# Feed-forward borders of a two-layer kernel: slots split at other times, sums of squares partly on GpSimd, chains in another order

## The reference, cut to what matters

```python
h = h + rmsnorm(mix, norm_mix_post)                 # end of the first layer's mixer
a = rmsnorm(h, norm_ffn_pre) @ w_ffn_in             # 1024 -> 2 x 2816
ap = jnp.pad(a, ((0, 0), (half, half), (0, 0)))
a = sum(ap[:, j:j + L] * conv_w[j] for j in range(CONV_W)) + conv_b
val, gate = a[..., :D_FF], a[..., D_FF:]
y = (jax.nn.gelu(gate, approximate=True) * val) @ w_ffn_out
h = h + rmsnorm(y, norm_ffn_post)
# second layer: u = rms_norm(h, norm_mix_2), u @ w_in_2 gives q, k, v of a windowed
# attention (q and k normalised per head and rotated), then the inputs of a recurrence
# (each a blend of a token with its two neighbours) and the gates
```

## Time and profile before

| what | value |
|---|---|
| median of 3 runs | 1938.53 us |
| lowest, highest | 1937.21, 1943.55 us |
| profiled execution, its own time | 1930.56 us |
| span of its trace | 1928.8 us |
| mean granted TensorE clock | 0.967 |
| ScalarE (ACT) busy | 649.8 us (34%) |
| GpSimd (POOL) busy | 88.5 us (5%) |
| DMA, mean over the span | 75 GB/s |

### The profile page before, as it was taken

The page is one execution under the profiler, slowest core; times in us unless marked ns, Lnnn a source line. Parts: engine busy times, 40 slices in busy tenths (PEclk is TensorE's granted clock), DMA queues, the critical chain, the costliest instruction groups (busy, mean ns, idle before and its releaser), DMA issues. The chain is left out here.

```text
span 1928.8 us, 38591 instructions
## 1 busy us (share of the span) xinstructions
PE 1771.6 (92%) x17168; PEld 1524.5 (79%) x17168; DVE 1020.2 (53%) x1527; ACT 649.8 (34%) x1064; POOL 88.5 (5%) x115
## 2 busy tenths in 40 slices
PE   6998999888999999989999998888579999999998
PEld 5888878888989989777677777777458888788877
DVE  3245765445635636546564555565656545353554
ACT  3242334433433423333334334333144322221232
POOL 7000000010000000100000000000001100000020
PEclk8999999979999999979999999999889999999999
DMA  5211120202222222221222200000052222223221
GB/s 163 88 67 45 63 81 23 90 23 88 87 88 88 96 101 88 90 80 66 77 83 71 77 24 4 4 4 10 2 229 88 88 89 106 90 88 109 88 88 66
DMA packets 29132, 144.57 MB, mean 75 GB/s; under 512 B 6315, under 2 KB 9659, under 8 KB 14380
## 3 DMA queue, kind: packets, MB, share of 16 engines
q1 hardware_dynamic: 24828, 133.58, 19.5%
q0 software_dynamic: 3856, 7.87, 1.5%
q10 hardware_dynamic: 288, 0.73, 0.1%
HBM read 134.82 MB, written 8.91 MB: 75 GB/s over the span
## 5 line engine op out<-in xcount | busy, mean ns | idle before, releaser
L228 DVE TENSOR_TENSOR w_w_lo<-w_w_raw,w_w_hi 128x2048 fp32r<-128x2048 f32 x66 | 151.3, 2292 | 185.6 <-ACT w_w_hi L215 185.2
L240 PE MATMUL f_bank<-u_hi,w_w_hi 128*128 128x258 f32 x704 | 204.1, 290 | 12.3 <-DVE w_w_lo L228 6.1
L241 PE MATMUL f_bank<-u_hi,w_w_lo 128*128 128x258 f32 x704 | 202.7, 288 | 0.0
L242 PE MATMUL f_bank<-u_lo,w_w_hi 128*128 128x258 f32 x704 | 201.2, 286 | 0.0
L240 PE MATMUL g_bank<-g_y_hi,g_w_hi 128*128 128x512 f32 x384 | 151.2, 394 | 16.7 <-DVE g_w_lo L228 12.5
L241 PE MATMUL g_bank<-g_y_hi,g_w_lo 128*128 128x512 f32 x384 | 150.3, 391 | 0.0
L242 PE MATMUL g_bank<-g_y_lo,g_w_hi 128*128 128x512 f32 x384 | 150.3, 391 | 0.0
L240 PEld LDWEIGHTS f_bank<-u_hi,w_w_hi 128*128 128x128 f32 x704 | 135.5, 193 | 13.7 <-issue 6.4
L215 ACT ACTIVATE g_w_hi<-g_w_raw 128x2048 fp32r<-128x2048 f32 x45 | 85.9, 1909 | 167.2 <-PE g_bank L242 165.2
L215 ACT ACTIVATE w_w_hi<-w_w_raw 128x2048 fp32r<-128x2048 f32 x66 | 125.7, 1905 | 32.0 <-PE f_bank L242 32.0
L242 PEld LDWEIGHTS f_bank<-u_lo,w_w_hi 128*128 128x128 f32 x704 | 136.5, 194 | 0.0
(11 more groups left out here) (512 smaller groups left out, 3956.6 us busy)
## 6 DMA issues: line engine op xcount, KB each, us to landing
g_w_raw<-in_w_ff SPq DMA_DIRECT2D x32, 1024.0 KB, 4.8
w_w_raw<-in_w_in SPq DMA_DIRECT2D x30, 1024.0 KB, 4.8
w_w_raw<-in_w_ffn_in SPq DMA_DIRECT2D x22, 1024.0 KB, 4.8
w_w_raw<-in_w_ffn_out SPq DMA_DIRECT2D x12, 1024.0 KB, 4.8
w_w_raw<-in_w_o SPq DMA_DIRECT2D x4, 1024.0 KB, 5.0
gate_pre<-rw_t POOLq DMA_DIRECT2D x16, 256.0 KB, 2.3
g_w_raw<-in_w_up SPq DMA_DIRECT2D x4, 1024.0 KB, 8.9
g_branch<-gate_pre SPq DMA_DIRECT2D x4, 1024.0 KB, 12.1
```

Source lines behind the costliest of these rows:

```text
L228: nc.vector.tensor_tensor(R.lo[:, r, 0:size], R.raw[:, r, 0:size], R.hi[:, r, 0:size].bitcast(F32), ALU.subtract).then_inc(R.split, 1)
L240: nc.tensor.matmul(out, w_hi, u_hi, start=start, stop=False)
L241: nc.tensor.matmul(out, w_lo, u_hi, start=False, stop=False)
L242: return nc.tensor.matmul(out, w_hi, u_lo, start=False, stop=stop)
```

## The change

- First border: slot 18 is copied to `hi` right after the root of the mixer's norm and split right after its diagonal, slot 19 after the second root and diagonal; the first hidden step splits nothing. The squares of both openings are added by GpSimd, and TensorE sums the seven added squares and the last square once: in the first opening after the first half tile of the second slot, in the second one before the last block's products. The first block's remainder comes before the second block's addition.
- Last hidden step: `lo` of the slot two ahead is made after `y_lo`. The first slot of the last down projection goes through all rows but the last for both tiles, then through the last row for both.
- Second border: slot 52 is copied after the root of the feed-forward norm, and split after the opening.
- Three one-column activations (Gelu, Sqrt, Exp) are added at places ahead of the first use of these functions.
- Attention: the second rotation moves behind the first mixed tile, and the last turned heads are read before the sixth mixed tile is blended.

The core of the diff (the new semaphores, the buffer of the sum in the second opening, and the calls that choose `out_slot` are left out):

```diff
+        h_sum = c[:].rearrange("p a b n -> p (a b n)")[:, 0:L]
...
+            add_squares(pool, nc, h_sq, h_sum, h_squared, h_added)
...
-                    pe.wait_ge(h_squared, k + 1)
-                    sum_tokens(pe, nc, C, bank[:, 3, :], h_sq[:, k % 2, :], T, TG, k == 0, k == KT - 1).then_inc(h_summed, 1)
...
+                        if m == 0 and half is outs[2 * r][0][0]:
+                            pe.wait_ge(h_added, KT - 1)
+                            sum_tokens(pe, nc, C, bank[:, 3, :], h_sum, T, TG, True, False)
+                            pe.wait_ge(h_squared, KT)
+                            sum_tokens(pe, nc, C, bank[:, 3, :], h_sq[:, (KT - 1) % 2, :], T, TG, False, True).then_inc(h_summed, 1)
...
+            def paired_slot(ph, q, r, rows, first):
+
+                pe.wait_ge(R.split, 2 * q + r + 1)
+                pe.wait_ge(R.tile_free, ph.c0)
+                for ks in (range(len(rows) - 1), [len(rows) - 1]):
+                    for m in range(2):
+                        out = whole[(r * 2 + m) % len(whole)][0][0]
+                        for k in ks:
+                            pe.wait_ge(y_done, first + k + 1)
+                            at = k * SLOT + m * P
+                            last = three_pass(nc, out, R.hi[:, r, at:at + P], R.lo[:, r, at:at + P],
+                                              y_hi[:, rows[k], :], y_lo[:, rows[k], :], k == 0, k == len(rows) - 1)
+                        if k == len(rows) - 1:
+                            last.then_inc(R.tile_done, 1)
+
+            def out_slot(g, j, q, r):
+                if g == 2 and isinstance(j, int) and j == 0:
+                    paired_slot(out[g], q, r, places[g], 8 * g)
+                else:
+                    gemm_slot(pe, nc, R, out[g], j, q, r, y_hi, y_lo, whole, places[g], ready=(y_done, 8 * g))
...
+            ahead_hi(act, nc, R, into[0].n0 + 1, into[0].c0)
             for k in range(KT):
                 act.wait_ge(added, k + 1)
                 nc.scalar.activation(u_hi[:, k, :], h[:, k, :], ACT.Copy, scale=column("ffn_pre", k)).then_inc(u_hi_done, 1)
                 if k >= 2:
-                    act.wait_ge(h_summed, k - 1)
+                    act.wait_ge(h_added, k - 1)
                 nc.scalar.activation(h_sq[:, k % 2, :], h[:, k, :], ACT.Square).then_inc(h_squared, 1)
-                if k == 4:
-                    ahead_hi(act, nc, R, into[0].n0 + 1, into[0].c0)
-            act.wait_ge(h_summed, KT)
+            act.wait_ge(h_summed, 1)
             nc.scalar.activation(stat[0:T, 1, :], bank[0:T, 3, 0:TG], ACT.Sqrt, scale=1.0 / D, bias=EPS).then_inc(tok_std, 1)
+            ahead_hi(act, nc, R, into[0].n0 + 2, into[0].done(0))
+            nc.scalar.activation(warm[:], C("ones")[:, 0:1], ACT.Gelu_apprx_tanh)
...
-                hi_ahead(act, nc, R, ph, j, q, r)
+                if not (isinstance(t, int) and t == 0):
+                    hi_ahead(act, nc, R, ph, j, q, r)
...
-                if t % 2:
+                if t % 2 and t < KT - 1:
                     j = t // 2
                     hi_ahead(act, nc, R, out[2], j, (out[2].n0 + j) // 2, (out[2].n0 + j) % 2)
+                if t == KT - 2:
+                    nc.scalar.activation(stat[:, 0, 0:1], C("ones")[:, 0:1], ACT.Sqrt)
...
+            ahead_lo(dve, nc, R, into[0].n0 + 1)
             dve.wait_ge(row_done, 1)
             dve.wait_ge(h_back, 16)
+
+            def remainder(k):
+                dve.wait_ge(u_hi_done, k + 1)
+                nc.vector.scalar_tensor_tensor(u_lo[:, k, :], h[:, k, :], column("ffn_pre", k),
+                                               u_hi[:, k, :].bitcast(F32), ALU.mult, ALU.subtract).then_inc(u_done, 1)
+
             for k in range(KT + 1):
                 if k < KT:
                     nc.vector.scalar_tensor_tensor(two_halves(acc[:, k, :]), two_halves(acc[:, k, :]), column("mix_post", k), row,
                                                    ALU.mult, ALU.mult).then_inc(scaled, 1)
+                    if k == 1:
+                        remainder(0)
                     dve.wait_ge(scaled, k + 1)
                     nc.vector.tensor_tensor(h[:, k, :], h[:, k, :], acc[:, k, :], ALU.add).then_inc(added, 1)
-                if k:
-                    dve.wait_ge(u_hi_done, k)
-                    nc.vector.scalar_tensor_tensor(u_lo[:, k - 1, :], h[:, k - 1, :], column("ffn_pre", k - 1),
-                                                   u_hi[:, k - 1, :].bitcast(F32), ALU.mult, ALU.subtract).then_inc(u_done, 1)
+                if k >= 2:
+                    remainder(k - 1)
...
-            ahead_lo(dve, nc, R, into[0].n0 + 1)
+            ahead_lo(dve, nc, R, into[0].n0 + 2)
...
-                lo_ahead(dve, nc, R, ph, j, q, r)
+                turned = isinstance(t, int) and t in (0, FT - 1)
+                if not turned:
+                    lo_ahead(dve, nc, R, ph, j, q, r)
...
+                if turned and t:
+                    lo_ahead(dve, nc, R, ph, j, q, r)
...
-                lo_ahead(dve, nc, R, out[g], j, q, r)
+                if not (g == 2 and isinstance(j, int) and j == 3):
+                    lo_ahead(dve, nc, R, out[g], j, q, r)
...
+            add_squares(pool, nc, x_sq, x_sum, x_squared, x_added)
...
+                        if k == KT - 1:
+                            pe.wait_ge(x_added, KT - 1)
+                            sum_tokens(pe, nc, C, bank[:, 2, :], x_sum, P, NB, True, False)
+                            pe.wait_ge(x_squared, KT)
+                            sum_tokens(pe, nc, C, bank[:, 2, :], x_sq[:, k % 2, :], P, NB, False, True).then_inc(x_summed, 1)
...
-                        pe.wait_ge(x_squared, k + 1)
-                        sum_tokens(pe, nc, C, bank[:, 2, :], x_sq[:, k % 2, :], P, NB, k == 0, k == KT - 1).then_inc(x_summed, 1)
...
+            ahead_hi(act, nc, R, qkv.n0 + 1, qkv.c0)
             for k in range(KT):
                 act.wait_ge(added, k + 1)
                 nc.scalar.activation(u_hi[:, k, :], x[:, k, :], ACT.Copy, scale=gain("mix2", k)).then_inc(u_hi_done, 1)
                 if k >= 2:
-                    act.wait_ge(x_summed, k - 1)
+                    act.wait_ge(x_added, k - 1)
                 nc.scalar.activation(x_sq[:, k % 2, :], x[:, k, :], ACT.Square).then_inc(x_squared, 1)
-            act.wait_ge(x_summed, KT)
+            act.wait_ge(x_summed, 1)
...
+            nc.scalar.activation(st[:, 118:119], C("ones")[:, 0:1], ACT.Exp)
...
+                if g == AHEAD - 1:
+                    read_heads(NB - 1)
                 taken_tile(g)
-                if g >= AHEAD - NB:
+                if AHEAD - NB <= g < AHEAD - 1:
...
+                    if k == 1:
+                        remainder(0)
                     dve.wait_ge(scaled, k + 1)
                     nc.vector.tensor_tensor(x[:, k, :], x[:, k, :], acc[:, k, 0:GRID], ALU.add).then_inc(added, 1)
-                if k:
-                    dve.wait_ge(u_hi_done, k)
-                    nc.vector.scalar_tensor_tensor(u_lo[:, k - 1, :], x[:, k - 1, :], gain("mix2", k - 1),
-                                                   u_hi[:, k - 1, :].bitcast(F32), ALU.mult, ALU.subtract).then_inc(u_done, 1)
+                if k >= 2:
+                    remainder(k - 1)
...
-            for j in range(2):
-                ahead_lo(dve, nc, R, qkv.n0 + j + 2)
+            for j in range(3):
+                ahead_lo(dve, nc, R, qkv.n0 + j + 1)
...
-            rotate(1)
             dve.wait_ge(row_read, 1)
             dve.wait_ge(mu_done, 2)
             dve.wait_ge(edges, 2)
             for g in range(AHEAD):
-                if g in (2, 3):
+                if g in (1, 2, 3):
```

More of the change, by code:

```diff
@@ L1310, in ffn_block @@
         sq_sum = a[:, 0, 0, 0:GRID]
-        sq_added = sem("sq_added")
+        sq_added, h_added = sem("sq_added"), sem("h_added")
+        h_sum = c[:].rearrange("p a b n -> p (a b n)")[:, 0:L]
+        warm = sb("warm", [P, 1])
         part = NEAR // 2
@@ L1381, in into_slot @@
                     gemm_slot(pe, nc, R, into[g], j, q, r, u_hi, u_lo, outs)
+            def paired_slot(ph, q, r, rows, first):
[16 more added lines that the diff above has]
+                    gemm_slot(pe, nc, R, out[g], j, q, r, y_hi, y_lo, whole, places[g], ready=(y_done, 8 * g))
             for g, (t0, count) in enumerate(groups):
                 each_slot(pe, into[g], lambda j, q, r, g=g: into_slot(g, j, q, r))
-                each_slot(pe, out[g], lambda j, q, r, ph=out[g], rows=places[g], ready=(y_done, 8 * g):
-                          gemm_slot(pe, nc, R, ph, j, q, r, y_hi, y_lo, whole, rows, ready=ready))
+                each_slot(pe, out[g], lambda j, q, r, g=g: out_slot(g, j, q, r))
         @block.scalar
@@ L1543, in attention_block @@
         diag = flat(s[:])[:, 0:GRID].rearrange("p (a b) -> p a b", a=NB)
-        x_sq = q_t[:, 0:2, :]
+        x_sq, x_sum = q_t[:, 0:2, :], q_t[:, 2, :]
         post, pre = st[:, 110:114], st[:, 114:118]
```

(11 more changed lines are left out.)

## The result

The changed kernel took 1911.32 us (median of 3 runs, 1908.49 to 1911.64), the kernel before 1938.53: ratio 0.9859, 95% interval [0.9829, 0.989], 27.2 us. Run again among the experiments it took 1909.88 us against 1934.25, ratio 0.9875 [0.9859, 0.9891], 24.4 us. The forecast was 1909, range 1896 to 1922.

A forecast was written before the change was run, and what follows sets the result against it. TensorE, busy 92% of the span, bounds the kernel with its standstills and low-clock stretches. Gains of 13.0+5.2+3.9+3.1+4.6 = 29.8 us, taken from the median 1938.53, give 1909 us; range 1896 to 1922.

The forecast's parts named there:

- Part 1(b): First opening: sums leave TensorE; GpSimd's addition costs VectorE's chain 0.42 us, giving a block every 2.5 us.
- rival B: Both openings: each GpSimd addition costs VectorE's chain its whole 1.09 us; gain 19, 1919 us; chance 0.16.
- blocks at 3.2 us or more: Sign in the openings that the forecast is wrong, pointing to rival B or D.
- Part 1(c): First border: second slot starts at 426.4 instead of 438.27, gain 11.9; losses 0.5 for sums, 1.0 for low clock.
- Part 1(d): First border: slot 19 split before the row is read, removing the 2.71 wait and its start-up; gain 2.9 us.
- Part 2: Last down-projection slots: late y_lo and slot 48's split covered, four slots in 32.7 instead of 37.9 us; gain 5.2.
- Part 3: Statistics behind the last down projection: first sum to first scaled tile 4.5 instead of 8.4 us; gain 3.9.
- Part 4: Second opening: 25.4 instead of 28.6 us, with a new 2.3 us wait for slot 52's split; gain 3.1.
- Part 5: Attention rotations: pause 0.8 instead of 3.58 us, heads read earlier, less 1.1 for a new pause; gain 4.6.
- Rival A: Openings: GpSimd takes nothing from VectorE and the clock rises early; gain 38, 1901 us; chance 0.18.
- C: Rival: late splits at slots 20 and 48, VectorE bounds the mixed tiles; gain 24, 1914 us; chance 0.13.
- D: Rival: GpSimd starved, openings become serial at 5.2 us a block; 14 us slower, 1952 us; chance 0.03.

The follow-up runs named there:

- the best: Changed kernel with ScalarE's squares before its rounded parts and slot 52's low part split right after the second opening's last remainder: 1906.54 us, again 1906.89.

## Why the prediction was right or wrong

The time fell 2 us from the forecast, and that nearness is in part luck. I counted the gain from the first median of before, 1938.53; its three later medians are 1932.58, 1934.25 and 1935.56, and from those 29.8 us would have led to 1902.8 to 1905.8, against the 1909.88 and 1911.32 measured. The sum was 4.1 us too high at the end of the attention stage, with misses of both signs behind it, and 3.3 more went after it.

**Part 1(b), GpSimd's price per block.** This is the mis-sized term. I took 0.42 from the earlier trace rows and gave a block 2.5 us. Without the additions the block was 2.11 in the first opening and 2.07 in the second; with them TensorE's blocks after the second start 3.1 us apart in the mean in the first opening (price 1.0), and VectorE's in the second alternate between 2.36 and 3.07 (mean price about 0.6). Single blocks reach rival B's price (3.26 less 2.11 is 1.15); as a mean over both openings it lies between mine and B's. The two openings cost 5.0 and 3.9 us, where I had put about 3 each. Of the prediction's signs, "blocks at 3.2 us or more" came for half of the blocks of the first opening.

The nearest row was the wrong guide: how long VectorE is held depends on how much of GpSimd's instruction is left when its own would start. The trace of before shows it at the very rows that I read. The remainder of 1.17 started at 1478.17, 0.63 us before GpSimd's addition ended (1475.99 + 2.81), and 1.17 is these 0.63 and 0.54. In the changed opening ScalarE's copy and square bring GpSimd's start exactly onto VectorE's addition in three of the six additions, and whoever loses waits for the whole of the other's. The rule of the Trainium skill ("SBUF — State Buffer", Who interferes with whom), that the shared pair is an exclusive lock and that the order of issue decides who blocks, says what the rows show: 1.31 and then 0.56 where GpSimd is first. Its sum, VectorE's two two-input operations and GpSimd's addition one after the other (0.71, 0.76 and 1.31 in these rows), is 2.8 us a block, nearer than mine.

**Part 1(c), the second slot.** The start-up wait and the low stretch went as said; the first tile with the two sums took 10.0 us (I said 9.9), and the 1.0 that I set aside for a return of the low clock was not needed: the products behind the sums take 0.28.

**Part 1(d), slot 19.** TensorE did gain the 2.71 and its start-up, but 1.8 us came out in that step (2.0 by the last down projection), since behind the row VectorE is the bound: in the first hidden step it never waits for TensorE, only 0.7 to 0.9 us at a time for ScalarE's turns in its chain. In the changed kernel the step from the first slot's rms product to the second's is 8.86 us (439.70 to 448.56), before it was 10.61 (447.67 to 458.28). What counts there is the 2.29 us of splitting taken out of VectorE's chain, less what it waits for ScalarE in its place. The rest TensorE hands back at its next meeting with that chain, the first down projection, where it waits 2.83 us (2.02 before) and starts 0.1 us after VectorE has read the bank. The first border gave 10.1 us to the last down projection, for 13.0.

**Part 2.** 5.2 us, as said. I took the whole stretch against its time at full rate, and so counted the low clock behind the wait with it; but in the experiment's theory I gave the pair 3 to 3.5 us of it, and it makes 1.9. The rest is VectorE's order: 1.7 less wait, and 1.5 because the clock then stays up.

**Part 3.** 2.7 for 3.9. The chain was right (root 2.48 us behind the first sum's start, the reciprocal at once); the spread stayed at the low clock, 2.07, where I had assumed 1.04. In six of the experiments' traces it took 1.16, and 1.68 in the second trace of the changed kernel itself, so the clock there differs between executions of one kernel. The table load was worth 0.3 us at most.

**Part 4.** 1.2 for 3.1: 0.5 until the first product and 0.7 until slot 52. The wait at slot 52 came as predicted (2.06, forecast 2.3). About half of the difference is GpSimd's price again (3.9 measured, about 3 allowed). The other 0.9 is there without the additions too: that opening takes 23.4 us to slot 52, and my 25.4 less my price of seven blocks is 22.5.

**Part 5.** 6.7 for 4.6 (5.2 in the second trace of the changed kernel): the wait went as said (0.82 left, forecast 0.8), and the pause of 2.9 us with the clock behind it, for which I took off 1.1, came as 1.89 us without. The first scores' low stretch went as well: from the first probabilities to the fourth it is 13.6 us against 17.6 (15.2 in the second trace). The old order put back costs 6.8 to 8.3 us in the traces, so my 4.6 looks too small.

**After it, 3.3 us lost.** Nothing of the recurrence is changed, and no wait for a transfer is longer there than before. The windows tell it (the same stretch of before and of after, the granted clock third from the right):

```profile
1195.00:1210.40 15.40, 11.94 (x531) 10.65 (x522) 12.03 (x23) 4.45 (x11) 0.00 (x0) 1.00 0.02 4
...
1350.60:1377.50 26.90, 20.73 (x703) 18.50 (x705) 15.88 (x37) 2.45 (x5) 0.00 (x0) 1.00 0.01 4
```

```profile
1168.20:1186.20 18.00, 13.02 (x529) 11.80 (x522) 12.43 (x24) 4.32 (x11) 0.00 (x0) 0.91 0.01 4
...
1324.40:1353.70 29.30, 22.04 (x703) 19.91 (x705) 15.94 (x37) 2.45 (x5) 0.00 (x0) 0.94 0.01 3
```

The same work takes 2.6 and 2.4 us longer where the clock was 0.91 and 0.94. From the last probabilities to the end took 808.2 us in the trace of before, and between 809.0 and 818.0 in the twelve others, 811.6 and 811.9 in those of the changed kernel, 816.0 and 814.2 in those of the best. How low the clock goes in such stretches differs between traces of one kernel, so part of it is chance. Whether all is stays open: all twelve are longer than the one of before, and with one trace of before it can't be told from a lucky one. Its time, 8.0 under the median of before, speaks for a lucky one.

Rival A's 2.1 us blocks came only without the additions, C's late splits at slots 20 and 48 never, D's serial opening never: ScalarE's square never waited for GpSimd. It is GpSimd that stood, 1.95 us at a time, for the square.

## What to carry over

Work handed to GpSimd beside VectorE costs VectorE what is left of GpSimd's instruction whenever its own two-input operation falls due inside it: twelve additions of 1.3 us cost 8 to 9 us here. Reckon with up to the full length, then ask which operation of VectorE reads PSUM and start GpSimd's there, by moving the instruction that feeds it. When a wait of TensorE is taken away ahead of a stage whose VectorE is already saturated, count what leaves VectorE's chain, not the bracket. And a split that must follow a chain of statistics belongs into the gap in which that chain waits for TensorE: here it took 2.9 to 3.9 us out of the stage in the traces, and 2.1 out of the time, for one moved call.

## What the runs showed of the hardware

- VectorE and GpSimd settle into a pattern that a tie decides. In one trace of the changed kernel GpSimd's addition wins it and VectorE's blocks are 3.25 us; in the other VectorE's wins it and they alternate between 2.42 and 3.15 (openings of 31.5 and 30.5 us).
- Where only wide products ran, they were at the high clock 3.3 to 5.2 us after the opening's first one (ten traces; 413.4 after 408.2 in the changed kernel's first). With one-column sums between them it took 12 to 13 us in the kernel that keeps all other edits, and 16 to 17 in the kernel before and the one with its first border.
- The same wait of TensorE, 2.83 us before the first down projection, is followed by 19 us with a mean granted clock of 0.91 and 1.00 in the two traces of the changed kernel and 0.82 in the one with the squares first. Over that place the first falls 1.4 us behind the second, and the last 2.8. Before it and after it the low parts of the hidden blocks keep their distance in these three traces within 0.03 us, up to the last down projection: all that they differ by over 330 us arises at that one place.
